# A transformer pair on one core: the moving tiles h and ax spaced out by 64 bytes a pair, the weight ring put on a 512-byte boundary

## What is computed

```
h = rms_norm(x);  proj = h @ w_in                      # 2048 deep
y = attention(proj), delta_net(proj)
x += (gate * (y1 @ w_up_nsa) + gate * (y2 @ w_up_dn)) @ w_o
h = rms_norm(x);  x += (silu(h @ w_gate) * (h @ w_up)) @ w_down    # 2048 -> 5632 -> 2048
... the second block: w_in_2, w_out_2, ffn_w_gate_2, ffn_w_up_2, ffn_w_down_2 in the same manner
out = rms_norm(x)
```

## Time and profile before

| what | value |
|---|---|
| median of 2 runs | 2855.6 us |
| span of the profiled execution | 2854.1 us |
| what lies around the span, against the median | 1.5 us |
| TensorE matmul busy | 2791.8 us (98%) |
| VectorE busy | 2051.3 us (72%) |
| ScalarE busy | 1363.8 us (48%) |
| GpSimd busy | 479.0 us (17%) |
| share of TensorE in the chain that ended last | 89% |
| read from HBM | 469.80 MB |

### The profile page before, as it was taken

The page is one execution under the profiler, slowest core; times in us unless marked ns, Lnnn a source line. Parts: engine busy times, 40 slices in busy tenths (PEclk is TensorE's granted clock), DMA queues, the critical chain, the costliest instruction groups (busy, mean ns, idle before and its releaser), DMA issues.

```text
span 2854.1 us, 41789 instructions
## 1 busy us (share of the span) xinstructions
PE 2791.8 (98%) x16404; PEld 2428.2 (85%) x16404; DVE 2051.3 (72%) x3158; ACT 1363.8 (48%) x2043; POOL 479.0 (17%) x526
## 2 busy tenths in 40 slices
PE   8999999999999999999999999999989999999998
PEld 7888888888888888888888888878778888888887
DVE  7987787766766666656657889878777777667655
ACT  6453455455554544444446545434354444434434
POOL 2111011110111111001002734511021111001101
PEclk9999999999999999999999999999999999999999
DMA  6444334455555555555556433321445555555555
GB/s 227 163 156 162 112 124 131 144 190 187 192 186 191 187 190 190 188 190 192 188 179 212 162 112 128 101 67 52 148 146 187 191 187 190 191 190 188 192 177 162
DMA packets 132243, 474.63 MB, mean 166 GB/s; under 512 B 14672, under 2 KB 14928, under 8 KB 131792
## 3 DMA queue, kind: packets, MB, share of 16 engines
q1 hardware_dynamic: 132048, 471.96, 50.0%
HBM read 469.80 MB, written 2.10 MB: 165 GB/s over the span
## 4 chain that ended last, share of the span: by engine, by line
PE 89%; DVE 5%; ACT 3%; POOL 1%; issue 1%; DMA 0%; SPq 0%; DVEq 0%; ACTq 0%; POOLq 0%
PE ps L893 88%; DVE ringl L1859 1%; DVE U L1859 1%; ACT high L1399 1%; POOL U L2540 1%; DVE xT L1859 1%; PE ps L896 1%; ACT hr L1399 0%; ACT U L1399 0%; POOL U L2613 0%; DVE U L1868 0%; ACT U L1412 0%; DMA xT<-in_x_dram 0%; DVE hx L1859 0%; DVE U L2056 0%
## 5 line engine op out<-in xcount | busy, mean ns | idle before, releaser
L893 PE MATMUL ps<-hr,high 128*128 128x512 f32 x4672 | 1508.0, 401 | 19.4 <-DVE ringl L1859 17.2
L1859 DVE TENSOR_TENSOR ringl<-ring,high 128x1024 fp32r<-128x1024 f32 x880 | 1080.5, 1230 | 424.5 <-ACT high L1399 423.8
L1399 ACT ACTIVATE high<-ring 128x1024 fp32r<-128x1024 f32 x880 | 914.4, 1041 | 635.8 <-PE ps L893 626.5
L893 PEld LDWEIGHTS ps<-hr,ringl 128*128 128x128 f32 x4672 | 880.0, 188 | 205.6 <-issue 1.4
L893 PE MATMUL ps<-hr,ringl 128*128 128x256 f32 x4672 | 920.6, 278 | 0.0
L893 PEld LDWEIGHTS ps<-hr,high 128*128 128x128 f32 x4672 | 721.9, 189 | 29.4 <-issue 15.1
L893 PE MATMUL ps<-yur,high 128*128 128x512 f32 x2176 | 684.3, 395 | 10.2 <-DVE xT L1859 6.7
L2540 POOL TENSOR_TENSOR U<-U,rs 128x256 f32<-128x256 f32 x292 | 263.0, 901 | 1701.3 <-DVE U L1859 1682.0
L893 PEld LDWEIGHTS ps<-yur,ringl 128*128 128x128 f32 x2176 | 409.4, 188 | 90.8
L1399 ACT ACTIVATE U<-ps 128x256 f32<-128x256 f32 (+3 forms) x481 | 172.7, 371 | 601.2 <-PE ps L893 575.6
L893 PE MATMUL ps<-yur,ringl 128*128 128x256 f32 x2176 | 430.3, 279 | 0.0
(11 more groups left out here) (178 smaller groups left out, 1255.0 us busy)
## 6 DMA issues: line engine op xcount, KB each, us to landing
ring<-in_w_dram SPq DMA_DIRECT2D x870, 512.0 KB, 3.3
ring<-in_w_dram SPq DMA_DIRECT2D x32, 256.0 KB, 3.3
xT<-in_x_dram SPq DMA_DIRECT2D x3, 512.0 KB, 8.1
out_dram<-hx SPq DMA_DIRECT2D x3, 512.0 KB, 2.8
cst<-in_cst_dram SPq DMA_DIRECT2D x1, 1374.5 KB, 12.5
yT<-in_lora_dram SPq DMA_DIRECT2D x1, 1024.0 KB, 7.8
xT<-in_x_dram SPq DMA_DIRECT2D x2, 256.0 KB, 4.7
U<-in_lora_dram SPq DMA_DIRECT2D x1, 512.0 KB, 5.8
```

Source lines behind the costliest of these rows:

```text
L893: return e.matmul(out, l, r, start=start, stop=stop)
L1399: return e.activation(out, i, ACT.Copy, scale=scale)
L1859: return e.tensor_tensor(out, a, b, op)
```

## The change

The ring now begins on a multiple of 2,048 bytes (`onto`), `high` behind it, and `hx`/`hr` behind `high`. Pair t // 2 of the tiles of `hr` begins 64 bytes (APART, 16 words) later for each pair ahead of it, so that the offsets of the 8 pairs are 0, 64, ... 448. `U` is placed so that the word 256 in it lies on a multiple of 2,048 bytes; `ax` begins 64 bytes behind that and is spaced in the same way: 16 pairs at 64, 128, ... 1,024. By the sizes, `yT` comes to 147 x 512 bytes behind the ring's start (ring and high 40,960, `hr` 32,768 + 448, `rs` 1,088), so that tiles in `yT` and `U` have the offset 0 in place of 64, and the high parts at dn0 the offset 192 in place of 256. `U` is 640 words shorter. Slices of the big arrays become lists of tiles; `ring_slot` and `high_slot` give the same places as the formulas that they replace. No instruction is added or taken away, and no wait.

```diff
+APART = 16
...
+        def onto(n, past=0):
+
+            while (base + 4 * (place[0] + past)) % n:
+                place[0] += 16
+
+        def ring_slot(m):
+            return (m % RING) * BLK
+
+        def high_slot(k):
+            return (k % HIGH) * BLK
...
         xT_ = sb("xT", 16 * SEQ)
-        h_at = place[0]
-        hx_ = sb("hx", 32 * SEQ)
+        onto(2048)
         ring_at = place[0]
         ring = sb("ring", RING * BLK)
         ringl = sb("ringl", RING * BLK, F32R, at=ring_at)
         high = sb("high", HIGH * BLK, F32R)
+        h_at = place[0]
+        hx_ = sb("hx", 32 * SEQ + 7 * APART)
         rs_ = sb("rs", SEQ + 16)
         y_at = place[0]
         yT_ = sb("yT", 16 * SEQ)
+        onto(2048, 256)
         u_at = place[0]
...
-        hr = sb("hr", 32 * SEQ, F32R, at=h_at)
+        hr = sb("hr", 32 * SEQ + 7 * APART, F32R, at=h_at)
...
-        hx, hxr = [shaped(a[:, :], 16, 2, SEQ) for a in (hx_, hr)]
-        hhF, hlF, hh, hl = hx[:, :, 0, :], hx[:, :, 1, :], hxr[:, :, 0, :], hxr[:, :, 1, :]
-        axr = shaped(yur[:, u_at - y_at + 256:u_at - y_at + 256 + 64 * SEQ], 32, 2, SEQ)
-        ah, al = axr[:, :, 0, :], axr[:, :, 1, :]
-        alF = shaped(U_[:, 256:256 + 64 * SEQ], 32, 2, SEQ)[:, :, 1, :]
-        flat = shaped(hx_[:, :], 32, SEQ)
+        def halves_of(ap, at, n):
+
+            return [shaped(ap[:, a:a + 2 * SEQ], 2, SEQ) for a in (at + 2 * SEQ * t + APART * (t // 2) for t in range(n))]
+
+        hxr = halves_of(hr, 0, 16)
+        hh, hl = [a[:, 0, :] for a in hxr], [a[:, 1, :] for a in hxr]
+        axr = halves_of(yur, u_at - y_at + 256 + APART, 32)
+        ah, al = [a[:, 0, :] for a in axr], [a[:, 1, :] for a in axr]
+        alF = [a[:, 1, :] for a in halves_of(U_, 256 + APART, 32)]
+        flat = shaped(hx_[:, 0:32 * SEQ], 32, SEQ)
...
-        ar.at = mark1 + 64 * SEQ
+        ar.at = mark1 + 64 * SEQ + 16 * APART
...
-                    return axr[:, 16 * (u.key[1] % 2) + k, :, :]
-                return hxr[:, k, :, :]
+                    return axr[16 * (u.key[1] % 2) + k]
+                return hxr[k]
```

More of the change, by code:

```diff
@@ L932, in moving @@
                     at = 16 * (u.key[1] % 2) + k
-                    return ah[:, at, :], al[:, at, :]
+                    return ah[at], al[at]
                 if u.kind == "uq":
@@ L937, in moving @@
                     return ckvT[:, k, :], None
-                return hh[:, k, :], hl[:, k, :]
+                return hh[k], hl[k]
             def ready(u, k):
@@ L978, in main @@
                             e.wait_ge(ndve.sem, ndve.after("B", u.kind[3:]))
-                        at = (m % RING) * BLK + off
-                        g = (order[m] % HIGH) * BLK + off if m in order else 0
+                        at = ring_slot(m) + off
+                        g = high_slot(order[m]) + off if m in order else 0
                         first, ends = n == 0, n == len(u.parts) - 1
@@ L1405, in taken_in @@
                 else:
-                    copy(hh[:, t, :], xT[:, t, :], scale=C(tag, t, t + 1)).then_inc(mact.sem, mact.inc("hh", tag, t))
+                    copy(hh[t], xT[:, t, :], scale=C(tag, t, t + 1)).then_inc(mact.sem, mact.inc("hh", tag, t))
                 if t >= 2:
@@ L1526, in evac2 @@
                     e.wait_ge(mdve.sem, mdve.after("v", f, t))
-                    copy(ah[:, at, :], alF[:, at, :]).then_inc(mact.sem, mact.inc("ah", f, t))
+                    copy(ah[at], alF[at]).then_inc(mact.sem, mact.inc("ah", f, t))
             def tanh_of(u):
@@ L1543, in split @@
                 n = blocks[m][2] * len(blocks[m][3])
-                o, g = (m % RING) * BLK, (k % HIGH) * BLK
+                o, g = ring_slot(m), high_slot(k)
                 e.wait_ge(s_ring[m % RING], 16 * (m // RING + 1))
@@ L1555, in main @@
                     for t in range(a, a + n):
-                        copy(hh[:, t, :], xT[:, t, :], scale=C("norm1", t, t + 1)).then_inc(mact.sem, mact.inc("hh", "norm1", t))
+                        copy(hh[t], xT[:, t, :], scale=C("norm1", t, t + 1)).then_inc(mact.sem, mact.inc("hh", "norm1", t))
                     if a + n in (2, 8, 12):
@@ L1872, in low_of @@
                 e.wait_ge(mact.sem, mact.after("hh", tag, t))
-                stt(hl[:, t, :], xT[:, t, :], C(tag, t, t + 1), hh[:, t, :], MUL, SUB).then_inc(mdve.sem, mdve.inc("hl", tag, t))
+                stt(hl[t], xT[:, t, :], C(tag, t, t + 1), hh[t], MUL, SUB).then_inc(mdve.sem, mdve.inc("hl", tag, t))
             def inverse_root(tag):
@@ L1952, in evac1 @@
                     e.wait_ge(mpool.sem, mpool.after("sc", u.i))
-                    stt(alF[:, at, :], tb[:, t % 4, :], 0.5, ub[:, t % 4, :], MUL, MUL).then_inc(mdve.sem, mdve.inc("v", f, t))
+                    stt(alF[at], tb[:, t % 4, :], 0.5, ub[:, t % 4, :], MUL, MUL).then_inc(mdve.sem, mdve.inc("v", f, t))
                 elif u.kind == "up" and key[0] == 1:
@@ L1965, in evac2 @@
                     e.wait_ge(mact.sem, mact.after("ah", f, t))
-                    tt(al[:, at, :], alF[:, at, :], ah[:, at, :], SUB).then_inc(mdve.sem, mdve.inc("al", f, t))
+                    tt(al[at], alF[at], ah[at], SUB).then_inc(mdve.sem, mdve.inc("al", f, t))
             def tb_of(u):
@@ L1977, in split @@
                 n = blocks[m][2] * len(blocks[m][3])
-                o, g = (m % RING) * BLK, (order[m] % HIGH) * BLK
+                o, g = ring_slot(m), high_slot(order[m])
                 e.wait_ge(hi.sem, hi.after(m))
@@ L2659, in load @@
                 n = blocks[m][2] * len(blocks[m][3])
-                slot = (m % RING) * BLK
+                slot = ring_slot(m)
                 if m >= RING:
```

## The result

The changed kernel takes 2871.47 us (2870.77 to 2872.18), the kernel before 2855.60 (2855.46 to 2855.73). The ratio is 1.0057, with a 95% interval from 1.0039 to 1.0074. I had forecast 2845; the time lies inside my range of 2795 to 2890, but on the other side of no change.

A forecast was written before the change was run, and what follows sets the result against it. TensorE's matmul stream was taken to bound the kernel. Terms of -13.7 (h), +0.4 (ax) and +2.6 (yT and U) sum to -10.7 us against the profiled 2854.1, whose span lies 1.5 under the median: forecast 2845 us, range 2795 to 2890.

The forecast's parts named there:

- What bounds the kernel: Whole kernel: TensorE, busy for 98% of the span, sets the time; the other engines have room for a 5% faster stream.
- Addresses matter by the offset to the weights: Matmul pairs: the moving tile's offset to the weights sets the price, 697 ns at 0, 690 at 64, by 16 in 700.
- the case that offsets do not matter: Rival for the whole kernel: the offset between the operands may not count, nothing moves, 2856 us; chance 0.18.
- yT and U, +2.6 us: Tiles of yT and U: all 384 pairs come from offset 64 to 0, each 6.7 ns dearer.
- w_up_dn: Its 64 pairs, high parts now at 192 and no longer 256, were taken to cost the same 6.7 ns more.
- h, -13.7 us: Gate and up projections: 2,044 of 2,336 pairs leave offset 0 and cost 690.5 ns, 6.7 ns less each.
- ax, +0.4 us: Down projections: 64 of 512 pairs go from offset 64 to 0, 6.7 ns dearer each; the third lot stays.
- The slower one: Rival for down projections and h at 128 and more: wide offsets cost w_up_dn's 706 ns, 2881 us; chance 0.20.
- What would show it: Gate and up timeline: a period of 8 pairs, one as dear as now, mean 691 ns; wo rises from 690 to 697.

The follow-up runs named there:

- ring_192: The kernel before with one line added: ring and all behind it begin 192 bytes later, putting h at offset 64 modulo 256; 2840.49 us, ratio 0.9949.
- high_192_on: The changed kernel's layout without steps, high 192 bytes further than ring: h at 0 to ring, 64 to high, ax 64 and 128; 2872.92 us.
- step_h_only: The changed kernel's layout with the 64-byte steps in h alone, ax, yT and U held at 64; 2864.79 us against 2855.88.
- ring_192_dn: ring_192 with dn0 16 words later, so the high parts of w_up_dn lie at offset 320; 2840.16 us, ratio 0.9947.

## Why the prediction was wrong

*What bounds the kernel*: right. TensorE's stream sets the time, no wait was added, the other engines did not change.

*Addresses matter by the offset to the weights*: right. yT and U, moved from offset 64 to 0, rose to the price of 0, and ring_192 shows both halves: the same address of its own with another offset changes the price of h, another address with the same offset does not change that of ax. I had given 0.18 to the case that offsets do not matter. The rule of the Trainium skill, page "TensorE: Matmul & The Clock Gate", section "Part 2: What happens when you issue a matmul", that a weight load takes no read bandwidth from the running matmul, does not give this stream's times: equal shapes cost 690 to 705 ns according to where the loaded weights lie (ax in high_192_on). Whether it is read bandwidth that is lost, no run here shows.

*yT and U, +2.6 us*: right in the price where their pairs run in a long row (wo), 696.0 against my 697. In w_up_nsa, whose units stand between units with h, 8 pairs went only from 695 to 699, since in the kernel before they already paid for a step. *w_up_dn*: its 8 pairs go from 706 to 700 ns, where I took 6.7 more; over its 64 pairs that is 0.4 us less in place of 0.4 more.

*h, -13.7 us*: **this step failed.** "I take 690.5 ns, the row of the nearest offset": the pairs off 0 cost 700, 701 and 697.5, and those at 0, which I had left at 697, cost 707. Two things are in this. First, 64 is the best of the eight offsets tried and so no stand-in for the others: with the held prices the mean is 694.5, so h would have gained 2.5 ns a pair and not 5.9. Second, and larger, the steps: 701.9 less 694.5 is 7.4 ns a pair. A step makes pairs behind it dearer, and here there is one at every pair: the same four offsets without steps between them (the held runs) do not cost it, and steps of 256 bytes, which are none modulo 256, do not either. -2.5 and +7.4 make +4.9, and 702.1 less 697.2 was measured. My sum priced every pair by its own offset alone and had no term for the order of the offsets, though the trace of the kernel before showed one in w_up_nsa, at 572.71 us. How the 7.4 is shared among the pairs (10 ns over the held price at 0 and at 64, 4 at 128 and at 192) is measured and not explained. Of the 2,336 pairs, the 408 in the first 440 us added nothing in the changed kernel: the first matmul of yur starts at 439.8 before and at 439.6 after. Why is open, for these pairs are not free in general: in ring_192 the same matmul starts at 436.8, 3.0 us earlier. The other 1,928 by 4.7 ns (701.9 less 697.2) are 9.1 us, and the run with steps in h alone has 8.9.

*ax, +0.4 us*: failed in the same step, and worse, since ax came from the best offset: 704 pairs by 11.3 ns (701.8 less 690.5) are 8 us by the stretches. With yT and U at the stretches' prices that makes 10 us, against 7.0 in the whole time. Added up from start to start over all pairs of yur, the traces of the changed kernel and of step_h_only are 7.2 us apart: the down projections 6.8, wo 0.8, wout 0.4, and w_up 0.9 less. So the stretches' prices were too much for some stages, and nothing is missing.

*The rivals.* The slower one ended nearest (2881 against 2871), and its sign came, a mean of h over 702 ns (702.1). That was luck: it priced wide offsets by w_up_dn, whose 706 was a mixture of two offsets, while held still they cost 690 to 697. *What would show it*: I asked for a period of 8 pairs with one as dear as now, and it was 4 pairs, with none as cheap as 690.

What stays open is what happens inside TensorE. Shown is that the price of a pair depends on where its moving tile lies against both weight tensors modulo 256 bytes, and on the offsets of the pairs ahead of it, three of them behind a step from 0 to 64. Not shown, and only my reading, is that the reads of weights and moving operand collide, and that the one stream keeps a lead or a lag against the other for a few pairs. Nor is there a rule that gives the price of a step or of two offsets in one pair.

## What to carry to other kernels

When matmuls of one shape cost different amounts in different stages with no wait between them, compare where their operands lie to one another before looking at engines. Measure each offset held still before mixing them: here the best one, reached by one line of padding, gave 0.5%, while spreading over all of them lost 0.6%. A price read from one arrangement is no price of its parts once their order changes.

## What the runs showed that I had not expected

A pair of matmuls has a memory: the same pair at the same offset cost 697 ns in a steady stream and 707 where the pairs ahead lay at another offset. After a step from 0 to 64 the settling takes three pairs, about 2.1 us. And the dependence has a period of 256 bytes, seen in four places: 0 and 256 in the changed kernel (707 both), steps of 256 (697.0), h at 320 in ring_192 (690.0), the high parts at 320 in ring_192_dn (690).
